# One core, two network blocks at 256 tokens: another division of the first row norm and of the last gate

## The chip, the cores and the metric

The kernel runs on one NeuronCore of a Trainium2 chip. The metric is the device time of one launch in microseconds (us); lower is better. Five engines matter: TensorE (PE, with its weight loads PEld), VectorE (DVE), ScalarE (ACT), GpSimd (POOL) and the queue that issues most transfers (SP).

## The reference, cut to what matters

Two networks run one after the other on x, 256 tokens of 1024 numbers in f32. The first block mixes a stick-breaking attention with a gated recurrence and has a feed-forward part; the second has two layers (gated linear attention, then differential attention), each with a feed-forward part and a gated addition. Only the very first and the very last step are touched by the change:

```python
def rmsnorm(x, g):
    y = x * lax.rsqrt(jnp.mean(x * x, axis=-1, keepdims=True) + EPS)
    return y * g

u = rmsnorm(x, norm1_g) @ w_in                 # the first product
...
gate = sigmoid(rms_norm(h, ple_norm[1]) @ ple_w_gate[1])
out = h + gate * (p[1] @ ple_w_proj[1])        # the last step
```

## The kernel before, in words

**Weights.** All weights are f32 and stream through SBUF in chunks of 128 x 2048 numbers (1 MB), in the order of the list CHUNKS. There are three slots. For each chunk ACT makes a high part (`hi`, L1041, a copy rounded to TensorE's fast format) and DVE a low part (`lo`, L1622, chunk minus high part). Each product is then three: high by high, high by low, low by high (`mm3`, over `mm` at L360). SP reloads a slot when the high and the low part of its old chunk exist (L2432). Chunk 0 comes in four pieces of 128 x 512, chunk 1 in two.

**Activations.** Tokens lie in two blocks of 128 rows. For a product they are turned: PE transposes a 128 x 128 block of each token block into PSUM (`turn_step`, L368), ACT copies the high part of it to X or O (`turn_hi`, L1050) and DVE computes the low part (`turn_lo`, L1634). A chunk's product goes over eight k blocks, each with one turned block.

**Start.** ACT issues the transfers of the identity and of a small table and loads its function table. Meanwhile PE runs 16 warm-up products of the identity with itself (each an f32 product of two loads). When a half of x lands, ACT squares it in two operations of 512 columns with a row sum (`row_square`, L1056; x0 is token block 0, x1 token block 1). The sums go through a ladder of tiny steps between DVE and ACT (`rows_rstd`, `rstd_y`, `rstd_r`; L1660, L1655, L1063, L1065, L1641, L1643, L1645). Then DVE scales token block 0 (L1719) and ACT token block 1 (L1098), the first 512 columns of each; ACT makes the high part of piece 0 of chunk 0, waits for the turning of k block 0, copies it, scales the other 512 columns (L1102), and goes on with copies and pieces in turn. DVE waits for that high part, makes the low part, scales its other 512 columns (L1722), and makes X's low parts.

**End.** The last four chunks are the gate's weights. `toks` computes one chunk: for each k block both token blocks, all in one PSUM bank, 48 products; the semaphore `gemm` rises after the last. ACT then takes the sigmoid of both token blocks (L1447), DVE multiplies with the projected p (L2150) and adds to H (L2152), each in one operation over both token blocks (128 x 512), and SP writes 256 columns of all tokens to the output (L2441), 256 KB.

Each engine's program is written out by hand in its order; a wait holds up everything behind it on its engine.

Of the kernel before, what the change touches and what calls it, by code (L numbers as in the profile page):

```python
# [10 lines left out]
ALU = mybir.AluOpType  # L11
ACT = mybir.ActivationFunctionType
# [170 lines left out]
hg_sig hg_lf hg_kq hg_one hg_ln hg_d hg_acc hg_ed hg_ex hg_p hg_s hg_acc2 hg_o  # L183
gates mg mg_hi mg_lo ff_b ff_ev ff_sq ff_hi ff_lo n1_r pn_r nm1_r bgh fin_m fin_r fin_h
gz gl_qk gl_l gl_m gl_abs gl_one gl_scan gl_c gl_e gl_z gl_s gl_u gl_ua gl_w gl_x gl_o gl_r8 gla_ev
sw_b sw_g sw_u sw_t sw_s sw_w sw_hi sw_lo p_hi p_lo ple_pw ple_g ple_gg ple_h
df_ev df_sq df_r df_kn df_tr df_qk df_sc df_mx df_e df_a df_ta df_at df_o df_l df_lx df_tab df_dsq df_ap df_dt df_thi df_tlo""".split()


# [111 lines left out]
def v3(ap, a):  # L301
    return ap.rearrange("p (a b) -> p a b", a=a)
# [52 lines left out]
def tensor_program(e, m):  # L355
# [88 lines left out]
    def toks(c, bank, ops, norm=None, ks=range(8)):  # L444
        w = m.weights(c)
        if ks[0] == 0:
            ready(c)
        for k in ks:
            if norm:
                ahead(norm, k)  # L450
            for tb in range(2):
                i = mm3(PS[:, bank, tb * 256:tb * 256 + 256], [x[:, k, tb * 128:tb * 128 + 128] for x in ops],
                        [x[:, k, :] for x in w], k == 0 and tb == 0, k == 7, True)
        if ks[-1] == 7:
            i.then_inc(s["gemm"], 1)
# [36 lines left out]


    e.wait_ge(s["d_idn"], 16)
    for _ in range(16):
        mm(PS[:, 3, 0:128], ident, ident, True, True)


# [319 lines left out]
    def swiglu(layer):  # L818
# [3 lines left out]
        for i in range(12):  # L822
# [22 lines left out]
            if i >= 1:  # L845
# [5 lines left out]
                else:  # L851
                    down_last(down_at(layer, 10), half_slot(ring, 10), 0, [4, 5, 6, 7], f"pn{layer}",
                              lambda: e.wait_ge(s["sw_w"], f0 + 11))

    def ple(layer):
        r0 = 16 if layer == 0 else 24
        for n in range(4):
            if n == 1:
                e.wait_ge(s["res"], r0)
            toks(AT[f"ple_w_gate{layer}"] + n, 3 + n, m.pair("OX"[layer]), f"pn{layer}" if n == 0 else None)  # L860
            if layer == 0 and n >= 1:
                h_step("nm1", 2 * n - 2)
                h_step("nm1", 2 * n - 1)
# [164 lines left out]
def scalar_program(e, m):  # L1028
# [58 lines left out]
    e.dma_start(m.CON[:, 0:nc0], m.io["const"][:, 0:nc0]).then_inc(s["d_idn"], 16)  # L1087
    e.dma_start(m.SML[:, 0:8], m.io["small"][:, 0:8]).then_inc(s["d_g1"], 16)
    e.preload_act_table_set(LOGEXP)
    for tb in range(2):  # L1090
        e.wait_ge(s[f"d_x{tb}"], 16)
        for n in range(2):
            row_square("n1", tb, n)
    rstd_y("n1")
    e.wait_ge(s["n1_r"], 1)
    r1 = m.sc("n1.r")[:, 1:2]
    H, HS = m.tok(m.H), m.tok(m.HS)
    act(HS[:, 1, 0:512], H[:, 1, 0:512], ACT.Copy, scale=r1).then_inc(s["n_hsa"], 1)  # L1098
    hi(0, 0)
    e.wait_ge(s["d_g1"], 16)  # L1100
    turn_hi("n1", 0)
    act(HS[:, 1, 512:1024], H[:, 1, 512:1024], ACT.Copy, scale=r1).then_inc(s["n_hsa"], 1)  # L1102
# [333 lines left out]
    def ple(layer):  # L1436
        g, pn, r = v3(m.ar(3584, 2048), 2), f"pn{layer}", m.sc(f"pn{layer}.r")
        new_residual(5 if layer else 3, pn)
        rstd_y(pn)
        e.preload_act_table_set(SIGMOID)  # L1440
        for n in range(4):
            c = AT[f"ple_w_gate{layer}"] + n
            hi(c + 2)
            e.wait_ge(s["gemm"], c + 1)
            e.wait_ge(s["pn_r"], layer + 1)
            for tb in range(2):
                i = act(g[:, tb, 256 * n:256 * n + 256], PS[:, 3 + n, 256 * tb:256 * tb + 256], ACT.Sigmoid,  # L1447
                        scale=r[:, tb:tb + 1])
            i.then_inc(s["ple_g"], 1)
            if layer == 0 and n >= 1:  # L1450
                turn_hi("nm1", 2 * n - 2, 2 * n - 1)
                if n == 2:
                    row_square("nm1", 0, 0)
                    row_square("nm1", 1, 0)
        e.preload_act_table_set(LOGEXP)
# [151 lines left out]
def vector_program(e, m):  # L1607
# [56 lines left out]
    def rows_rstd(name, sem=None):  # L1664
        mean_square(name, rows_sum(name), 1.0 / 1024)
        return rstd_r(name, sem)
# [47 lines left out]
            i.then_inc(s["ns_ap"], 1)  # L1714


    r = rows_rstd("n1", ("n1_r", 1))
    H, HS = m.tok(m.H), m.tok(m.HS)
    e.tensor_scalar(HS[:, 0, 0:512], H[:, 0, 0:512], r[:, 0:1], None, ALU.mult).then_inc(s["n_hsd"], 1)  # L1719
    e.wait_ge(s["d_g1"], 16)  # L1720
    lo(0, 0)
# [417 lines left out]
    def ple(layer, r):  # L2139
        pw, g = m.ar(1536, 2048), m.ar(3584, 2048)  # L2140
        pn = f"pn{layer}"
        new_residual(5 if layer else 3, [4, 5, 6, 7], r)
        rows_rstd(pn, ("pn_r", layer + 1))
        for n in range(4):
            c = slice(256 * n, 256 * n + 256)
            lo(AT[f"ple_w_gate{layer}"] + n + 2)
            gg = v3(g, 2)[:, :, c]
            e.wait_ge(s["ple_pw"], 4 * layer + 4)
            e.wait_ge(s["ple_g"], 4 * layer + n + 1)
            e.tensor_tensor(gg, gg, v3(pw, 2)[:, :, c], ALU.mult).then_inc(own.up(), 1)  # L2150
            settled()
            e.tensor_tensor(H[:, :, c], H[:, :, c], gg, ALU.add).then_inc(s["ple_h"], 1)  # L2152
            if layer == 0 and n >= 1:
                turn_lo("nm1", 2 * n - 2, 2 * n - 1)
# [260 lines left out]
def sync_program(e, m):  # L2415
# [20 lines left out]
            src = io[name][k1 * 128:(k1 + kn) * 128, n0:n0 + nn].rearrange("(k p) n -> p k n", p=128)  # L2436
            e.dma_start(m.chunk(c, j)[0].rearrange("p (k n) -> p k n", k=kn), src).then_inc(s[landed(c, j)[0]], 16)
    o_rows = m.out.rearrange("(b p) d -> p b d", p=128)
    for n in range(4):
        e.wait_ge(s["ple_h"], 5 + n)  # L2440
        e.dma_start(o_rows[:, :, 256 * n:256 * n + 256], H[:, :, 256 * n:256 * n + 256]).then_inc(s["d_out"], 16)  # L2441
    e.wait_ge(s["d_out"], 64)


def program(nc, io, out):
# [74 lines left out]
```

## Time and profile before

| | us |
|---|---|
| median of 3 runs | 1082.48 |
| lowest and highest of them | 1080.42, 1082.62 |
| the profiled execution, its own time | 1080.15 |
| span of the profiled execution, first to last instruction | 1078.0 |
| DMA data read from HBM | 181.8 MB |

All rows that follow are of the one profiled execution; times in them count from the start of its span. The page gives the busy share of each engine and the chain of work that ended last. The chain view lists that chain in order of time: start, length, what. The timeline lists instructions in order: start, length, engine, line, operation, tiles and shapes, number of instructions merged, and in brackets the idle time in front and what ended it. The windows view gives, for each stretch, the busy time and number of instructions of each engine, the granted clock of TensorE (1.00 is full), the share of time in which the transfer engines are busy, and GB/s.

### The profile page before, as it was taken

How to read it: one execution, taken by the hardware profiler on the slowest of the kernel's cores; microseconds unless marked ns; L12 is line 12 of the kernel's file. 1: busy time of each engine (PE TensorE's matmuls, PEld its weight loads, DVE VectorE, ACT ScalarE, POOL GpSimd, SP SyncE). 2: the span in 40 equal slices, each digit the busy share in tenths (PEclk: the TensorE clock that was granted, in tenths of full speed). 3: DMA queues.
4: the chain of work that ended last, by engine and by line, in shares of the span. 5: the costliest groups of instructions: out<-in, count | busy, mean ns of one | idle time of the engine just before them, and what ended most of it. 6: DMA issues, size and time to landing. Idle time of an engine off the chain costs nothing.

```text
span 1078.0 us, 16570 instructions
## 1 busy us (share of the span) xinstructions
PE 1058.2 (98%) x6790; PEld 949.2 (88%) x6790; DVE 714.5 (66%) x819; ACT 598.7 (56%) x764; POOL 48.2 (4%) x51
## 2 busy tenths in 40 slices
PE   7999999999999999999999999999999999999998
PEld 7999999888888879998888888899998888888888
DVE  5557776756565666866566666667989676666564
ACT  6557544464444446756654544476686564444464
POOL 0000000020000000000102300010000100000010
PEclk9999999999999999999999999999999999999999
DMA  7835434546556455345455554645533446555641
GB/s 258 260 119 171 143 119 156 176 152 203 192 174 217 160 176 178 117 158 166 157 196 185 205 195 159 212 152 172 173 112 119 161 164 200 187 196 172 215 160 40
DMA packets 138298, 183.93 MB, mean 171 GB/s; under 512 B 4176, under 2 KB 122064, under 8 KB 138224
## 3 DMA queue, kind: packets, MB, share of 16 engines
q1 hardware_dynamic: 137776, 182.29, 50.9%
q8 instruction: 54, 0.88, 0.3%
q0 software_dynamic: 160, 0.52, 0.2%
q14 instruction: 20, 0.16, 0.0%
q10 hardware_dynamic: 288, 0.07, 0.0%
HBM read 181.82 MB, written 1.05 MB: 170 GB/s over the span
## 4 chain that ended last, share of the span: by engine, by line
PE 91%; DVE 4%; ACT 2%; issue 1%; DMA 1%; ACTq 0%; SPq 0%; DVEq 0%
PE PS L360 89%; PE PS L368 2%; DVE WL L1622 1%; ACT WH L1041 1%; DMA RAW<-in_gla_w_in_dram 0%; DMA H<-in_x_dram 0%; ACT HS L1056 0%; ACT AR L1056 0%; DVE SC L2212 0%; DVE HS L1711 0%; ACT SC L1063 0%; ACT SC L1065 0%; ACT X L1050 0%; DVE SC L1655 0%; DVE AR L2150 0%
## 5 line engine op out<-in xcount | busy, mean ns | idle before, releaser
L1622 DVE TENSOR_TENSOR WL<-RAW,WH 128x2048 fp32r<-128x2048 f32 (+1 forms) x170 | 379.0, 2231 | 149.8 <-ACT WH L1041 149.3
L1041 ACT ACTIVATE WH<-RAW 128x2048 fp32r<-128x2048 f32 (+1 forms) x175 | 325.5, 1863 | 92.4 <-PE PS L360 88.8
L360 PE MATMUL PS<-WH,X 128*128 128x256 f32 (+1 forms) x1264 | 312.0, 333 | 0.7 <-issue 0.5
L360 PE MATMUL PS<-O,WH 128*128 128x512 f32 (+2 forms) x880 | 265.3, 362 | 0.7 <-DVE AR L2012 0.7
L360 PEld LDWEIGHTS PS<-WH,X 128*128 128x128 f32 x1264 | 216.7, 190 | 24.8 <-issue 1.3
L360 PE MATMUL PS<-X,WH 128*128 128x256 f32 (+1 forms) x864 | 218.0, 331 | 1.8 <-DVE X L1634 1.0
L360 PE MATMUL PS<-WL,X 128*128 128x256 f32 (+1 forms) x632 | 208.8, 330 | 0.0
L360 PE MATMUL PS<-O,WL 128*128 128x256 f32 x744 | 203.2, 281 | 0.0
L360 PEld LDWEIGHTS PS<-O,WH 128*128 128x128 f32 (+1 forms) x880 | 155.0, 187 | 25.5 <-DVE AR L2012 0.9
L360 PE MATMUL PS<-X,WL 128*128 128x256 f32 x608 | 167.5, 281 | 0.0
L360 PEld LDWEIGHTS PS<-X,WH 128*128 128x128 f32 x864 | 144.9, 190 | 16.8 <-ACT X L1050 1.2
L360 PE MATMUL PS<-WH,O 128*128 128x256 f32 (+1 forms) x624 | 149.3, 327 | 0.6 <-issue 0.6
L360 PEld LDWEIGHTS PS<-O,WL 128*128 128x128 f32 x744 | 140.0, 188 | 3.1
L360 PEld LDWEIGHTS PS<-WL,X 128*128 128x128 f32 x632 | 120.0, 190 | 11.3
L360 PEld LDWEIGHTS PS<-X,WL 128*128 128x128 f32 x608 | 115.3, 190 | 1.8
L360 PEld LDWEIGHTS PS<-WH,O 128*128 128x128 f32 x624 | 105.6, 190 | 10.0 <-ACT O L1520 0.7
L360 PE MATMUL PS<-WL,O 128*128 128x256 f32 (+1 forms) x312 | 101.1, 324 | 0.0
L1410 ACT ACTIVATE AR<-PS 128x512 f32<-128x512 f32 x44 | 26.3, 597 | 116.3 <-PE PS L360 116.3
L360 PEld LDWEIGHTS PS<-WL,O 128*128 128x128 f32 x312 | 59.4, 190 | 4.7
L360 PE MATMUL PS<-AR 128*128 128x128 f32 (+7 forms) x512 | 59.2, 300 | 1.4 <-ACT AR L1504 1.1
L360 PEld LDWEIGHTS PS<-AR 128*128 128x128 f32 (+3 forms) x512 | 50.2, 177 | 6.8 <-issue 1.8
L2368 POOL TENSOR_TENSOR WL<-RAW,WH 128x2048 fp32r<-128x2048 f32 x5 | 23.1, 4620 | 533.6 <-ACT WH L1041 533.6
(197 smaller groups left out, 774.2 us busy)
## 6 DMA issues: line engine op xcount, KB each, us to landing
RAW<-in_ffn_w_in_dram SPq DMA_DIRECT2D x44, 1024.0 KB, 5.1
RAW<-in_w_ff_dram SPq DMA_DIRECT2D x32, 1024.0 KB, 5.4
RAW<-in_ffn_w_out_dram SPq DMA_DIRECT2D x22, 1024.0 KB, 5.1
RAW<-in_w_in_dram SPq DMA_DIRECT2D x20, 1024.0 KB, 5.1
RAW<-in_gla_w_in_dram SPq DMA_DIRECT2D x12, 1024.0 KB, 5.5
RAW<-in_diff_w_in_dram SPq DMA_DIRECT2D x12, 1024.0 KB, 5.2
RAW<-in_ple_w_gate_dram SPq DMA_DIRECT2D x8, 1024.0 KB, 5.2
RAW<-in_w_out_dram SPq DMA_DIRECT2D x4, 1024.0 KB, 5.0
```

Of the source, the lines that this page charges most:

```text
L360: return e.matmul(o, l, r, start=start, stop=stop, skip_group_check=skip)
L368: return e.transpose(o, i, m.con("ident", slice(0, k))[:, 0:k])
L1041: act(high, raw, ACT.Copy).then_inc(s["w_hi"], 1)
L1410: act(v3(m.ar(5632 + 1024 * x + 512 * (i % 2), 512), 2), PS[:, 2 * x:2 * x + 2, 256:512], ACT.Copy).then_inc(s["sw_b"], 1)
L1622: e.tensor_tensor(low, raw, high.bitcast(F32), ALU.subtract).then_inc(s["w_lo"], 1)
L2368: e.tensor_tensor(low, raw, high.bitcast(F32), ALU.subtract).then_inc(s["w_lop"], 1)
```

## The change

It has four parts at the start and one at the end.

1. PE runs 10 warm-up products instead of 16.
2. ACT squares only token block 0. DVE squares token block 1 in two operations (H x 1.0 x H with a row sum) once x1 has landed, waits for its own results, and goes into the ladder.
3. ACT makes the high part of piece 0 of chunk 0 after its last step of the ladder and in front of the scaling, where it came behind the scaling.
4. The last gate chunk of the last layer (n == 3) is computed by token block: all eight k blocks of token block 0 into bank 6, then of token block 1 into bank 7. A new semaphore, ple_t, rises after the first. Each block has its own sigmoid, its own product and addition of 256 columns on DVE, and its own output transfer of 128 KB. ACT's last table load falls away.

```diff
@@ tensor
     e.wait_ge(s["d_idn"], 16)
-    for _ in range(16):
+    for _ in range(10):
         mm(PS[:, 3, 0:128], ident, ident, True, True)
+    def last_gates():
+        c, ops = AT["ple_w_gate1"] + 3, m.pair("X")
+        w = m.weights(c)
+        ready(c)
+        for tb in range(2):
+            for k in range(8):
+                i = mm3(PS[:, 6 + tb, 0:256], [x[:, k, 128 * tb:128 * tb + 128] for x in ops],
+                        [x[:, k, :] for x in w], k == 0, k == 7)
+            i.then_inc(s["ple_t" if tb == 0 else "gemm"], 1)
@@ scalar
-    for tb in range(2):
-        e.wait_ge(s[f"d_x{tb}"], 16)
-        for n in range(2):
-            row_square("n1", tb, n)
+    e.wait_ge(s["d_x0"], 16)
+    ss = m.sc("n1.ss")
+    act(m.tok(m.HS)[:, 0, 0:512], m.tok(m.H)[:, 0, 0:512], ACT.Square, accum_out=ss[:, 0:1])
+    act(m.tok(m.HS)[:, 0, 512:1024], m.tok(m.H)[:, 0, 512:1024], ACT.Square, accum_out=ss[:, 2:3]).then_inc(s["row_sq"], 1)
     rstd_y("n1")
+    hi(0, 0)
     e.wait_ge(s["n1_r"], 1)
...
     act(HS[:, 1, 0:512], H[:, 1, 0:512], ACT.Copy, scale=r1).then_inc(s["n_hsa"], 1)
-    hi(0, 0)
...
+            if layer == 1 and n == 3:
+                for tb in range(2):
+                    e.wait_ge(*((s["gemm"], c + 1) if tb else (s["ple_t"], 1)))
+                    act(g[:, tb, 768:1024], PS[:, 6 + tb, 0:256], ACT.Sigmoid, scale=r[:, tb:tb + 1]).then_inc(s["ple_g"], 1)
+                return
@@ vector
+    H, HS = m.tok(m.H), m.tok(m.HS)
+    e.wait_ge(s["d_x1"], 16)
+    for n in range(2):
+        c = slice(512 * n, 512 * n + 512)
+        e.scalar_tensor_tensor(out=HS[:, 1, c], in0=H[:, 1, c], scalar=1.0, in1=H[:, 1, c], op0=ALU.mult, op1=ALU.mult,
+                               accum_out=m.sc("n1.ss")[:, 2 * n + 1:2 * n + 2]).then_inc(own.up(), 1)
+    settled()
     r = rows_rstd("n1", ("n1_r", 1))
...
+            if layer == 1 and n == 3:
+                for tb in range(2):
+                    gg = v3(g, 2)[:, tb, c]
+                    e.wait_ge(s["ple_g"], 8 + tb)
+                    e.tensor_tensor(gg, gg, v3(pw, 2)[:, tb, c], ALU.mult).then_inc(own.up(), 1)
+                    settled()
+                    e.tensor_tensor(H[:, tb, c], H[:, tb, c], gg, ALU.add).then_inc(s["ple_h"], 1)
+                return
@@ sync
-    for n in range(4):
+    for n in range(3):
         e.wait_ge(s["ple_h"], 5 + n)
         e.dma_start(o_rows[:, :, 256 * n:256 * n + 256], H[:, :, 256 * n:256 * n + 256]).then_inc(s["d_out"], 16)
-    e.wait_ge(s["d_out"], 64)
+    for b in range(2):
+        e.wait_ge(s["ple_h"], 8 + b)
+        e.dma_start(o_rows[:, b, 768:1024], H[:, b, 768:1024]).then_inc(s["d_out"], 16)
+    e.wait_ge(s["d_out"], 80)
```

## Rows read from the trace of the kernel before

**Rows 1.** The page: busy time by engine; the chain by engine.
```profile
PE 1058.2 (98%) x6790; PEld 949.2 (88%) x6790; DVE 714.5 (66%) x819; ACT 598.7 (56%) x764; POOL 48.2 (4%) x51
...
PE 91%; DVE 4%; ACT 2%; issue 1%; DMA 1%; ACTq 0%; SPq 0%; DVEq 0%
```

**Rows 2.** The chain view, 0 to 30 us: start, length, what.
```profile
6.22 1.34 ACT HS L1056 x4
...
7.59 0.17 DVE SC L1660
...
9.76 0.53 ACT WH L1041
...
10.42 0.69 DVE WL L1622
...
11.51 0.41 DVE X L1634
...
12.01 0.95 PE PS L360 x6
...
18.53 1.24 DVE WL L1622
```

**Rows 3.** Windows view of the start, and the timeline of PE's weight loads.
```profile
5.00:8.20 3.20, 3.18 (x15) 3.18 (x16) 0.33 (x2) 2.70 (x9) 0.00 (x0) 1.00 1.07 358
8.20:10.10 1.90, 1.90 (x19) 1.90 (x19) 0.97 (x4) 1.26 (x3) 0.00 (x0) 1.00 1.10 354
10.80:12.00 1.20, 0.22 (x2) 0.02 (x1) 1.11 (x3) 1.20 (x3) 0.00 (x0) 1.00 1.10 347
...
5.02 5.15 PEld L360 LDWEIGHTS PS<-CON 128*128 128x128 f32 x32 [5.02 <-DMA CON<-in_const_dram]
10.09 0.69 PEld L368 LDWEIGHTS PS<-CON,HS 128*128 128x128 f32 x6
...
12.70 0.24 PEld L368 LDWEIGHTS PS<-CON,HS 128*128 128x128 f32 x2
```

**Rows 4.** Timeline of ACT at the start.
```profile
5.97 0.19 ACT L1056 ACTIVATION_READ_ACCUMULATOR HS<-H 128x1 f32 x1
...
9.04 0.72 ACT L1098 ACTIVATE HS<-H,SC 128x512 f32<-128x512 f32 x1 [0.62 <-DVE SC L1645]
9.67 0.61 ACT L1041 ACTIVATE WH<-RAW 128x512 fp32r<-128x512 f32 x1
10.69 0.47 ACT L1050 ACTIVATE X<-PS,SML 128x256 fp32r<-128x256 f32 x1 [0.40 <-PE PS L368]
...
13.21 0.47 ACT L1050 ACTIVATE X<-PS,SML 128x256 fp32r<-128x256 f32 x1 [0.20 <-PE PS L368]
```

**Rows 5.** Timeline of DVE at the start.
```profile
11.03 0.48 DVE L1722 TENSOR_SCALAR HS<-H,SC 128x512 f32<-128x512 f32 x1
```

**Rows 6.** DVE's groups by line and shape: count, busy us, mean ns, idle before.
```profile
L1973 DVE SCALAR_TENSOR_TENSOR AR<-AR 128x512 f32<-128x512 f32 x16 | 11.1, 692 | 0.5
...
L1783 DVE TENSOR_TENSOR O<-PS,O 128x256 fp32r<-128x256 f32 x4 | 1.7, 416 | 0.2 <-ACT O L1155 0.2
```

**Rows 7.** Timelines of ACT and DVE at the end.
```profile
1067.31 0.84 ACT L1447 ACTIVATE AR<-PS,SC 128x256 f32<-128x256 f32 x2 [4.92 <-PE PS L360]
1073.07 0.84 ACT L1447 ACTIVATE AR<-PS,SC 128x256 f32<-128x256 f32 x2 [4.92 <-PE PS L360]
...
1074.73 0.69 DVE L2152 TENSOR_TENSOR H<-H,AR 128x512 f32<-128x512 f32 x1
```

**Rows 8.** Transfers, 1074 to 1078: GB/s in 0.1 us slices; issues with time to landing.
```profile
GB/s 0 0 0 0 0 0 0 0 0 0 0 0 0 0 0 0 0 0 0 0 0 0 0 113 358 348 328 338 369 348 307 113 0 0 0 0 0 0 0 0
...
out_dram<-H SPq DMA_DIRECT2D x1, 256.0 KB, 2.1
```

**Rows 9.** Transfers issued from 1.6 to 2.0 us.
```profile
RAW<-in_w_in_dram SPq DMA_DIRECT2D x1, 256.0 KB, 5.3
```

**Rows 10.** Waits of SP over the whole span: us in total, times, longest.
```profile
SPq L2432 <- DVE WL L1622: 935.7, 163, 15.6
```

More of the change, by code:

```diff
@@ L185 @@
 gz gl_qk gl_l gl_m gl_abs gl_one gl_scan gl_c gl_e gl_z gl_s gl_u gl_ua gl_w gl_x gl_o gl_r8 gla_ev
-sw_b sw_g sw_u sw_t sw_s sw_w sw_hi sw_lo p_hi p_lo ple_pw ple_g ple_gg ple_h
+sw_b sw_g sw_u sw_t sw_s sw_w sw_hi sw_lo ple_t p_hi p_lo ple_pw ple_g ple_gg ple_h
 df_ev df_sq df_r df_kn df_tr df_qk df_sc df_mx df_e df_a df_ta df_at df_o df_l df_lx df_tab df_dsq df_ap df_dt df_thi df_tlo""".split()
@@ L859, in ple @@
                 e.wait_ge(s["res"], r0)
+            if layer == 1 and n == 3:
+                last_gates()
+                break
             toks(AT[f"ple_w_gate{layer}"] + n, 3 + n, m.pair("OX"[layer]), f"pn{layer}" if n == 0 else None)
@@ L1714, in norm_apply @@
             i.then_inc(s["ns_ap"], 1)
+    H, HS = m.tok(m.H), m.tok(m.HS)
[5 more added lines that the diff above has]
+    settled()
     r = rows_rstd("n1", ("n1_r", 1))
-    H, HS = m.tok(m.H), m.tok(m.HS)
     e.tensor_scalar(HS[:, 0, 0:512], H[:, 0, 0:512], r[:, 0:1], None, ALU.mult).then_inc(s["n_hsd"], 1)
@@ L2146, in ple @@
             lo(AT[f"ple_w_gate{layer}"] + n + 2)
+            if layer == 1 and n == 3:
+                for tb in range(2):
[5 more added lines that the diff above has]
+                return
             gg = v3(g, 2)[:, :, c]
```

## The prediction, made before the change was run

> **What bounds the kernel now.** I read the page first: PE is busy for 98% of the span, and the chain that ended last lies on PE for 91% of it [rows 1]. DVE (66%) and ACT (56%) have slack almost everywhere. So a microsecond can only be won where PE does not yet run or no longer runs, and this change touches those two places and no other. Then I read the chain of the first 30 us [rows 2]. PE's first product comes at 12.01. What leads there is the transfer of x (its second half is there at 6.22), ACT's squares, a ladder of tiny steps that ends at 9.04, the scaling of the rows (0.72) [rows 4], the high part of the first weight piece, its low part (10.42 to 11.11), DVE's second scaling and the first low part of the turned X (until 11.92). Two more things must be seen there, which the chain does not show. The 32 loads of the 16 warm-up products occupy PE from 5.02 until 10.17, and the first turning of X stands behind them at 10.09 [rows 3], although the later of the two scaled halves was there at 9.04 + 0.72 = 9.76 [rows 4]. And ACT, once it has scaled and copied the first high part, waits 0.40 us for that turning [rows 4].
>
> Last I read the end. The final gate chunk is through when ACT starts on it at 1073.07; then come two sigmoids, a product and an addition on DVE over both token blocks, and one 256 KB transfer [rows 7, 8]. From there to the end of the span are 1078.0 - 1073.07 = 4.93 us without a product, which nothing hides.
>
> **Terms at the start.** (a) Fewer warm-up products. Per product there are two loads. In the windows [rows 3] the loads begin 0.21 us apart until 8.2 and 0.11 us apart after it: 3.2 us / 15 intervals, and 1.9 us for 17 loads and a part of the turning. The granted clock of both windows reads 1.00, so the record does not show the change of level; the pace says 1.2 GHz ahead of 8.2 and 2.4 GHz behind it. 20 loads instead of 32: sixteen have begun by 8.2 (to 8.18, at 0.21), four more at 0.11 are through at about 8.75. PE is then free 1.4 us earlier, and the turning starts when the scaled halves are there.
>
> (b) Squares of token block 1 on DVE. Now ACT needs 1.34 us for them after 6.22 [rows 2]. On DVE an operation with two f32 inputs of 512 columns out of SBUF takes 0.69 us (L1973) [rows 6]. Operations of that kind follow one another every 0.6 us: 10.42 to 11.03 between the low part and the scaling [rows 2, 5]. Two make 0.61 + 0.69 = 1.30. No row of before shows DVE with a sum output, so the cost of that is bounded: nothing at the low end, 0.19 us each at the high end (ACT's own read of its sum [rows 4]). I take 0.08 each, half of a tiny DVE step of 0.17 [rows 2], since such a step is the nearest DVE row and half of it may overlap. That gives 6.22 + 1.30 + 0.16 = about 7.7, against 7.59 now: the ladder begins 0.1 us **later** (bounds -0.05 and +0.35). The move takes ACT off the path and puts DVE on it; it gains nothing by itself. Nothing else is queued on DVE at that time, and ACT finishes the other half at 5.97 + 0.19 = 6.16 [rows 4], hidden behind the arrival of x.
>
> One rule of the Trainium skill speaks against it. Our row shows a two-input f32 operation at 0.69 us, the full pace of one column per 1.07 ns. The Vector Engine (DVE) Microarchitecture Reference, section Points that are easy to get wrong, says that this kind of operation with two SBUF sources that aren't bf16 halves its throughput, because both read ports are taken. L1973 contradicts that without a sum; no row has it with one. It is a rival below.
>
> (c) The high part before the scaling. ACT idles 0.62 us ahead of the scaling; the copy takes 0.61 [rows 4] and the first weight piece has landed at about 1.7 + 5.3 = 7.0 [rows 9]. It fits into that hole, so it costs nothing and the scaling is not pushed back. It lets DVE make the low part right behind its scaling (9.5 to 10.2 instead of 10.42 to 11.11), and takes 0.6 us of DVE work away from before the first low part of X. If the hole were gone, it would cost at most 0.61.
>
> Sum at the start. The scaled halves are there at 9.76 + 0.1 = 9.86. In steady state ACT's copy of a turned block starts 0.5 us after the first load of that turning begins (12.70 to 13.21) [rows 3, 4]. So ACT starts at about 10.4 instead of 10.69: 0.3 earlier. The first product could come 0.5 earlier (X's low part is 10.9 to 11.4 instead of until 11.92). But behind it ACT runs scaling, copy, high part and copy with no wait between them: its next idle row is the one at 13.21 [rows 4]. That stretch begins with the copy at 10.69 and so moves by 0.3 only, and DVE's low parts follow it. So the third k block starts 0.3 earlier, and from there on PE's own pace decides. Gain at the start: **0.3 us** (bounds 0 from b's high end, 0.6 if the first product decides). It is kept until the end: chunk 1 waits for its low part, which DVE makes at 18.53 behind the last turned block [rows 2], SP waits for DVE's low parts before it reloads a slot (163 waits) [rows 10], and all of that shifts along.
>
> **Terms at the end.** The last chunk has the same 48 products at the same size, only sorted by token block; consecutive gates start 5.76 us apart (1067.31 and 1073.07) [rows 7], so each half is 2.88 us and PE ends as now. Token block 0's tail (below 2 us of ACT and DVE, then its transfer) starts at 1070.2 and lies beside the second half. Behind it remain: one sigmoid of 0.47 instead of the pair of 0.84, saving 0.37; a product and an addition of 256 columns, where the nearest row has 0.42 (L1783) [rows 6], instead of 0.69 each [rows 7], saving 2 x 0.27 = 0.54; and a transfer of half the size. The data of the 256 KB transfer move for eight slices of 0.1 us; issue to landing is 2.1 us [rows 8]. Half the bytes save up to 0.4, at least 0 if more than the moving was fixed; I take 0.4, because the eight slices run at a full 340 GB/s. Together 0.37 + 0.54 + 0.4 = **1.3 us** (bounds 0.9 and 1.3). The added wait of DVE on the second sigmoid has nothing queued behind it but its own two operations; SP's fifth output transfer waits behind the fourth, which is issued 2.9 us ahead and landed by then. The dropped table load (1.28 us, ends before the transfer) was hidden. DMA: Bandwidth & Descriptors in the Trainium skill, section Anatomy of one DMA, says most of a transfer's fixed part is the confirmation from the target and does not depend on size; 2.1 less 0.8 of moving agrees, and by that the saving is the moving part alone.
>
> **Sum.** 0.3 + 1.3 = 1.6 us. On the profiled execution: span 1078.0 - 1.6 = 1076.4, its own time 1080.15 - 1.6 = 1078.5 (2.15 us lie outside the span). The median of the runs is 1082.48, so 2.3 above the profiled one, though the lowest run, 1080.42, is close to it. Carried to the median: 1082.5 - 1.6 = **1080.9 us**. Less than 0.2% (2.2 us) cannot be told from no change here, and 1.6 is below it.
>
> **Rivals.**
> 1. *Clock rises later in most runs.* The end of 32 warm-up loads depends on when the pace changes, and the program does not choose that. At 0.21 throughout, they would end at 5.02 + 32 x 0.213 = 11.84 instead of 10.17, and the turning with them; 20 loads would end at 9.3, still before the scaled rows at 9.86. Each run of before in which the rise is late loses up to 1.7 more, the kernel after almost nothing. For it: three runs spread over 2.2 us, the profiled one lies at the bottom. Against: other work of a long kernel varies too, and late slow products cost both. Gain 1.6 to 3.3; with 3.3, 1079.2. Chance 0.36.
> 2. *DVE squares at half pace* (the skill's rule of above as a mechanism of this kernel). Each square would take 1.3 instead of 0.7, the ladder begins 1.25 late, all of the start with it: scaled rows at 11.0, product 0.6 later than before. 0.6 lost against 1.3 at the end: 0.7 gain, 1081.8. For it, only the rule; against it L1973 at 0.69. Chance 0.08.
> 3. *The end gives less than it says*: transfer of 128 KB as slow as 256 KB, or a wait of some tenths between the halves: 0.9 + 0.3, 1081.3. Chance 0.08.
> 4. *PE's clock falls back, and it gets slower.* Between 8.75 and the first product at 11.5 PE would do only the six turning loads (0.7 us). If it goes to 1.2 GHz there, a product of 256 columns costs about 0.23 instead of 0.12 (5.76 us / 48), by the ratio 0.21 to 0.11 of the loads: 0.11 lost each. A low stretch of 3.2 us as at the beginning eats 1.5 (1082.4, par); from 15 products on it is slower than before, from 34 on (3.8 us lost) by over 0.2%; all of chunk 0 gives 5.3 lost, 1086. Against it: between 10.8 and 12.0 PE does 0.22 us of work now and the products behind run at full pace. Chance 0.05.
>
> **How the numbers follow.** Forecast 0.43, rivals 0.36, 0.08, 0.08, 0.05. The forecast's own range is 1080.3 to 1081.9 (bounds of b and of the transfer); a tenth of its weight falls past 1080.3. Faster by over 0.2% (under 1080.3): 0.36 plus 0.05 = 0.41. Slower by over 0.2%: 0.05. Same: 0.54. The range that leaves out 2 in 10 cuts the outer part of rival 1 and all of rival 4: 1078.7 to 1082.3.
>
> **What would show it.** Right: 20 loads ending near 8.8, the turning's first load near 9.9, DVE's two squares over by 7.7, first product near 11.5, last sigmoid's start to end of span 3.6 to 3.7 instead of 4.93, and five output transfers of which the last is 128 KB. Wrong: squares of more than 0.75 each, the high part ending after the ladder, loads of 0.2 behind 12, a gap on PE between the last two halves, or a last transfer that takes 2.1 again.

## Result and profile after

| | kernel before | changed kernel |
|---|---|---|
| median of the runs, us | 1082.39 (20 runs, 1080.23 to 1083.93) | 1080.31 (19 runs, 1078.62 to 1080.70) |
| ratio of the changed kernel, 95% interval | | 0.9982 (0.9975 to 0.9989) |
| the profiled execution, its own time | 1080.15 | 1080.1 |
| its span | 1078.0 | 1078.0 |

One further run of the changed kernel took 2691 us and is left out. The gain is 2.08 us of the median (0.18%; by the interval 1.2 to 2.7 us). The prediction had 1080.9, and the interval leaves 1 out, though the gain is below the 0.2% that the prediction took to be the least that can be told from no change. Yet the two profiled executions are equally long, and that needs an explanation: by the steps of the prediction the span should have been 1.6 us shorter.

The page of the changed kernel, busy time by engine, stands beside [rows 1]. DVE has 1.6 us more, with its squares, and ACT 2.5 less. PE is busy 1.0 us **more** although it has twelve warm-up instructions less, which is a first sign that some of its products took longer.

```profile
PE 1059.2 (98%) x6778; PEld 949.9 (88%) x6778; DVE 716.1 (66%) x825; ACT 596.2 (55%) x759; POOL 48.2 (4%) x51
```

The chain of the changed kernel, 0 to 30 us (start, length, what), against [rows 2]:

```profile
6.87 0.70 DVE HS L1740 x3
...
7.60 0.17 DVE SC L1679
...
9.05 0.73 ACT HS L1113
...
9.92 0.42 PE PS L368 x2
...
10.43 0.48 ACT X L1064
...
11.53 0.94 PE PS L360 x6
```

The first product starts at 11.53 instead of 12.01. In PE's timeline the third k block starts at 13.69 instead of 13.95, and chunk 1 at 19.66 instead of 19.90: between these two executions the start has gained 0.24 us. The ladder begins at 7.60, where it was 7.59. The timelines of its engines show why (start, length, engine, line, operation, in brackets the idle time in front and what ended it): PEld, ACT, DVE.

```profile
5.05 4.26 PEld L360 LDWEIGHTS PS<-CON 128*128 128x128 f32 x20 [5.05 <-DMA CON<-in_const_dram]
9.89 0.64 PEld L368 LDWEIGHTS PS<-CON,HS 128*128 128x128 f32 x6 [0.57 <-DVE HS L1744]
```
```profile
8.34 0.61 ACT L1055 ACTIVATE WH<-RAW 128x512 fp32r<-128x512 f32 x1
9.05 0.72 ACT L1113 ACTIVATE HS<-H,SC 128x512 f32<-128x512 f32 x1
10.43 0.47 ACT L1064 ACTIVATE X<-PS,SML 128x256 fp32r<-128x256 f32 x1 [0.66 <-PE PS L368]
```
```profile
6.25 0.69 DVE L1740 SCALAR_TENSOR_TENSOR HS<-H 128x512 f32<-128x512 f32 x1 [6.25 <-DMA H<-in_x_dram]
6.87 0.08 DVE L1740 DVE_READ_ACCUMULATOR HS<-H 128x1 f32 x1
6.87 0.68 DVE L1740 SCALAR_TENSOR_TENSOR HS<-H 128x512 f32<-128x512 f32 x1
7.48 0.08 DVE L1740 DVE_READ_ACCUMULATOR HS<-H 128x1 f32 x1
```

PE no longer stands in front of the turning: it idles 0.57 us until the scaled rows exist. The loads took 0.21 us each nearly to the end here, so in this execution the clock rose about 1 us later than in that of [rows 3]. The high part (L1055) lies in the hole before the scaling. The squares take 0.69 and 0.68, each with 0.08 for its sum.

The end: the timelines of ACT and DVE, and the last transfer (issue to landing), against [rows 7, 8].

```profile
1071.56 0.47 ACT L1461 ACTIVATE AR<-PS,SC 128x256 f32<-128x256 f32 x1 [2.04 <-PE PS L360]
1074.43 0.47 ACT L1461 ACTIVATE AR<-PS,SC 128x256 f32<-128x256 f32 x1 [2.40 <-PE PS L360]
```
```profile
1074.94 0.43 DVE L2176 TENSOR_TENSOR AR<-AR 128x256 f32<-128x256 f32 x1 [1.99 <-ACT AR L1461]
1075.40 0.42 DVE L2178 TENSOR_TENSOR H<-H,AR 128x256 f32<-128x256 f32 x1
```
```profile
out_dram<-H SPq DMA_DIRECT2D x1, 128.0 KB, 1.7
```

From the last sigmoid to the end of the span are 1078.0 - 1074.43 = 3.57 us instead of 4.93: 1.36 gained. So 0.24 + 1.36 = 1.6 us are gained at the two ends, and yet the last sigmoid starts 1074.43 - 1073.07 = 1.36 us **later** than before. The middle, which the change does not touch, has lost 1.6 us. The windows view (busy time and number of instructions of PE, PEld, DVE, ACT, POOL, then granted clock, share of the transfer engines, GB/s) finds most of it, here for the changed kernel and then for the one before:

```profile
183.80:185.80 2.00, 0.20 (x2) 0.12 (x2) 2.00 (x5) 0.00 (x0) 0.00 (x0) 1.00 0.36 33
186.00:187.00 1.00, 1.00 (x9) 0.93 (x8) 0.34 (x1) 0.85 (x2) 0.00 (x0) 0.84 0.93 385
187.00:188.00 1.00, 1.00 (x7) 1.00 (x7) 0.54 (x2) 0.02 (x1) 0.00 (x0) 0.50 1.02 422
188.00:190.00 2.00, 2.00 (x11) 2.00 (x11) 1.06 (x2) 1.08 (x1) 0.00 (x0) 0.50 0.21 80
190.00:191.00 1.00, 1.00 (x10) 1.00 (x10) 0.28 (x2) 0.84 (x1) 0.00 (x0) 0.95 0.00 0
```
```profile
183.80:185.80 2.00, 0.35 (x3) 0.14 (x2) 2.00 (x5) 0.00 (x0) 0.00 (x0) 1.00 0.25 35
...
188.00:190.00 2.00, 2.00 (x19) 2.00 (x18) 1.28 (x2) 1.72 (x1) 0.00 (x0) 1.00 0.32 121
```

In both executions PE has almost nothing to do from 183.8 to 185.8: it waits 1.80 us for a low part of O that stands in DVE's program behind a weight chunk's low part (L1641 in the changed kernel). In the changed kernel's execution the granted clock then goes to 0.50 (1.2 GHz) from within the slice 186 to 187 until past 190 (0.16 / 0.5 + 3 + 0.05 / 0.5 = 3.4 us by the rows); 11 products go through in two microseconds instead of 19. DVE's operation L1943, which takes the next result, stands at 195.29, where its counterpart (L1918 of the kernel before) stands at 194.05: 1.24 later, though the start was 0.24 earlier. That is a loss of 1.48 us in this stretch; 0.12 are spread over the rest.

### The profile page after: what moved, and what is told of

The parts are those of the page before. It is cut to its first block, busy times and chain, and to the rows that moved or that the text cites. A ratio compares the mean times of both kernels' runs of the same rounds, so it can differ in the third digit from the quotient of the medians.

```text
span 1078.0 us, 16547 instructions
## 1 busy us (share of the span) xinstructions
PE 1059.2 (98%) x6778; PEld 949.9 (88%) x6778; DVE 716.1 (66%) x825; ACT 596.2 (55%) x759; POOL 48.2 (4%) x51
## 4 chain that ended last, share of the span: by engine, by line
PE 91%; DVE 4%; ACT 2%; issue 1%; DMA 1%; SPq 0%; DVEq 0%; ACTq 0%
PE PS L360 89%; PE PS L368 2%; DVE WL L1641 1%; ACT WH L1055 1%; DMA RAW<-in_gla_w_in_dram 0%; DMA H<-in_x_dram 0%; ACT AR L1070 0%; DVE SC L2245 0%; ACT X L1064 0%; DVE HS L1730 0%; ACT SC L1077 0%; ACT SC L1079 0%; DVE SC L1674 0%; DVE H L2185 0%; DVE AR L2183 0%
## 5 line engine op out<-in xcount | busy, mean ns | idle before, releaser
L1641 DVE TENSOR_TENSOR WL<-RAW,WH 128x2048 fp32r<-128x2048 f32 (+1 forms) x170 | 379.0, 2231 | 148.1 <-ACT WH L1055 147.7
L1055 ACT ACTIVATE WH<-RAW 128x2048 fp32r<-128x2048 f32 (+1 forms) x175 | 325.6, 1863 | 94.5 <-PE PS L360 89.8
```

The lines of the kernel that those rows point to most:

```text
L1055: act(high, raw, ACT.Copy).then_inc(s["w_hi"], 1)
L1641: e.tensor_tensor(low, raw, high.bitcast(F32), ALU.subtract).then_inc(s["w_lo"], 1)
```

## Experiments

All are edits of the changed kernel, and ratios are to the kernel before, timed on the same chip. Beside the median I give how the runs lie, since they lie in **groups** mostly 1.2 to 2.2 us apart, with the mean granted clock of the execution: the kernel before has them at about 1080.3 (clock 0.999 to 1.000), 1082.5 (0.997 to 0.998) and 1083.5 (0.997), the changed kernel at 1078.7 (5 of 19 runs, 1.000) and 1080.3 (14 of 19, 0.998). A mean of 0.999 need not be a low stretch among the products: in the kernel before's profiled execution the only one is behind PE's last product (0.57 from 1076 us on). Where two kernels are compared below, equal groups are compared. The experiments ran apart from the changed kernel's runs, on three chips; the kernel before ran beside each of them and has its fastest group at 1079.8 to 1080.7 every time.

### Start alone, end alone

e1 has the changed start and the old end; e2 the old start and the changed end.

```diff
# e1: the end back
-            if layer == 1 and n == 3:
-                last_gates()
-                break
...
# e2: the start back
-    for _ in range(10):
+    for _ in range(16):
...
```

> Only the parts at the start are made (10 warm-up products, squares of token block 1 on VectorE, the high part ahead of the scaling); the end is that of before. My theory: the gains add up and the start is the small one: 0.2 to 0.4 us under before among runs of equal mean granted clock, last sigmoid to end of span 4.93 as before. Rival (the late rise of the clock makes before's upper runs, which fewer warm-ups cure): 0.3 under before in its lower runs and 1.5 to 2 under it in its upper runs, so the start alone would give most of the 2.1 us by which the medians differ.

> Only the end is made (last gate chunk by token block, each with its own tail and transfer); the start is that of before. My theory: 1.3 us under before (0.9 on ACT and DVE, 0.4 on the transfer) among runs of equal mean granted clock; last sigmoid to end of span 3.6. The runs still fall into two groups some 1.7 to 2 us apart. Rival (clock at the start): 1.3 under before too, but then this kernel alone keeps an upper group as frequent as before's.

Measured: **e1** 1080.46 (12 runs), ratio 0.9990 (0.9981 to 0.9998); 8 runs at 1080.1 to 1080.5, 4 at 1081.5 to 1082.0. **e2** 1081.29 (11 runs), ratio 0.9993 (0.9984 to 1.0003); 2 runs at 1078.6 and 1079.2, 8 at 1080.8 to 1081.8, 1 at 1082.4. The kernel before on the same chip has 11 runs at 1079.9 to 1080.6, 13 at 1082.0 to 1082.9 and 3 at 1083.4 to 1083.6. PEld and ACT at the start, for e1 and then e2:

```profile
5.11 4.34 PEld L360 LDWEIGHTS PS<-CON 128*128 128x128 f32 x20 [5.11 <-DMA CON<-in_const_dram]
9.95 1.11 PEld L368 LDWEIGHTS PS<-CON,HS 128*128 128x128 f32 x6 [0.51 <-DVE HS L1736]
...
10.74 0.47 ACT L1061 ACTIVATE X<-PS,SML 128x256 fp32r<-128x256 f32 x1 [0.91 <-PE PS L368]
```
```profile
5.04 6.27 PEld L360 LDWEIGHTS PS<-CON 128*128 128x128 f32 x32 [5.04 <-DMA CON<-in_const_dram]
11.23 0.69 PEld L368 LDWEIGHTS PS<-CON,HS 128*128 128x128 f32 x6
...
11.83 0.47 ACT L1064 ACTIVATE X<-PS,SML 128x256 fp32r<-128x256 f32 x1 [1.53 <-PE PS L368]
```

The 32 loads of 16 warm-up products took 6.27 us in e2 and 5.15 in [rows 3], with the same program up to there. So the moment at which the clock rises is not the program's: that was the premise of rival 1, and it holds. In both of these executions it came late: the 20 loads of e1 took 0.21 us each to the end, and its six turning loads 1.11 us instead of 0.64. Then the first product starts at 12.92 in e2 and at 11.84 in e1, and chunk 1 at 21.05 and 19.97, 1.08 apart both times. With the rise at about 8.2 the kernel before has 12.01 and 19.90; with the rise at about 9.2 the changed kernel has 11.53 and 19.66. So fewer warm-up products protect against most of a late rise, not all of it: e1's chunk 1 is 0.07 later than that of the kernel before with its early rise.

The runs say the same of the start alone. e1's expectation of 0.2 to 0.4 us in equal groups fails in the fastest one: e1's runs (1080.1 to 1080.5) lie where those of the kernel before lie. In the next group they are about 0.8 lower. The end alone is 1.1 and 1.7 lower in e2's two fastest runs and about 1.1 in the next group. The end is worth what was said: from the last sigmoid to the end of the span are 1079.2 - 1075.63 = 3.6 us in e2 and 1078.4 - 1073.46 = 4.9 in e1.

### The parts of the start, one undone at a time

```diff
# e4_warm_16
-    for _ in range(10):
+    for _ in range(16):
# e7_warm_0
-    for _ in range(10):
+    for _ in range(0):
# e5_squares_back: ACT squares both token blocks, DVE none
-    e.wait_ge(s["d_x0"], 16)
...
+    for tb in range(2):
+        e.wait_ge(s[f"d_x{tb}"], 16)
+        for n in range(2):
+            row_square("n1", tb, n)
# e6_piece_back
-    hi(0, 0)
     e.wait_ge(s["n1_r"], 1)
...
     act(HS[:, 1, 0:512], H[:, 1, 0:512], ACT.Copy, scale=r1).then_inc(s["n_hsa"], 1)
+    hi(0, 0)
```

> The changed kernel with 16 warm-up products again. My theory: in an execution whose clock rises early (loads at 0.11 us from about 8.2) the 32 loads end near 10.2, the turning starts 0.3 late and the first product comes at 11.8 to 11.9 instead of 11.5. In one whose clock rises late, at 10.5 or after, the loads end at 11.3, and the first product comes at 12.9 as in the kernel with the end alone. Rival (the number of warm-up products doesn't matter because the scaled rows are late anyway): first product at 11.5 whenever the clock rises.

> The changed kernel without any warm-up product. It tells what the clock does to a start without them (my rival 4 in its strongest form). If the clock does not rise before the products: turning loads and the products of chunk 0 at half pace, 0.23 instead of 0.12 a product, for about 3 to 5 us, so the third k block starts 1 us later or more and the end 1.5 to 2.5 us later. If the clock were up anyway, nothing changes but PE's idle time ahead of 9.9.

> The changed kernel with all four squares on ACT again. My theory, after the changed kernel's trace (VectorE's squares were over at 7.56, as ACT's before): nothing moves; first tiny step at 7.59 to 7.60, turned copy at 10.4, first product at 11.5. My prediction of before had VectorE 0.1 later than ACT, by which this kernel would be 0.1 earlier. The high part of piece 0 is not pushed, because ACT is free from 7.6 on.

> The changed kernel with the high part of piece 0 behind the scaling again. My theory: ACT's turned copy still starts near 10.4, VectorE's low part of piece 0 goes back to 10.4 to 11.1 and its second scaling behind it, X's first low part to 11.4, first product near 12.0; but the third k block moves by 0.1 or less, because ACT's stretch behind the first copy is the same. So the last product comes 0 to 0.2 later. Rival (the low part is what leads): the whole 0.5 us is lost until the end.

| | median us (runs) | ratio, interval | chunk 1's first product in the profile |
|---|---|---|---|
| changed kernel | 1080.31 (19) | 0.9982 (0.9975 to 0.9989) | 19.66 |
| e4, 16 warm-up products | 1081.35 (8) | 0.9993 (0.9982 to 1.0004) | 20.33 |
| e7, none | 1080.86 (8) | 0.9993 (0.9982 to 1.0004) | 20.25 |
| e5, squares back on ACT | 1079.92 (8) | 0.9978 (0.9967 to 0.9989) | 19.86 |
| e6, high part back | 1079.77 (6) | 0.9985 (0.9971 to 1.0000) | 19.81 |

**e4**: its fastest group, 1079.3 and 1079.4, is 0.6 above the changed kernel's, its middle one (1081.1 to 1081.4) 0.9 above, and three runs at 1082.3 to 1082.5 lie in a third that the changed kernel lacks. The turning starts at 10.51, right behind the 32nd load, and the first product at 12.20. **e7**: without warm-up products the turning is in time (9.70), but six loads take 1.14 instead of 0.64 and the first products 0.63 a pair instead of 0.40, until about 13.3; the third k block and chunk 1 come 0.6 later, where 1 us or more was expected. Its runs are 4 at 1080.4 to 1080.6 (clock 0.999 to 1.000) and 4 at 1081.1 to 1081.6 (0.998), 1.8 and 0.9 above the changed kernel's groups; no row shows where the part of this that exceeds 0.6 is lost. Of the three numbers tried, ten lie between a queue that is too long and an engine that is still at half clock. **e5**: the ladder began at 7.63 in its profile, where the changed kernel has 7.60; the fastest runs, 1078.2 and 1078.8, lie by the changed kernel's. The 0.2 at chunk 1 belongs to a slower turning (0.81 for six loads), not to the squares. Moving the squares to DVE brings nothing and costs nothing that these runs resolve. **e6**: the low part of the first piece is at 10.39 instead of 9.46, the first product at 11.97, chunk 1 at 19.81, and the fastest group at 1078.8 to 1079.2: the moved high part is worth 0.15 us at chunk 1, up to 0.4 in the runs. (Its median is low because three of its six runs fell into the fastest group, where five of 19 did of the changed kernel; with so few runs a median says how they fell, and groups must be compared.)

### The last transfer in one piece

```diff
# e8_one_transfer
-    for n in range(3):
-        e.wait_ge(s["ple_h"], 5 + n)
+    for n in range(4):
+        e.wait_ge(s["ple_h"], 5 + n + (n == 3))
...
-    for b in range(2):
-        e.wait_ge(s["ple_h"], 8 + b)
-        e.dma_start(o_rows[:, b, 768:1024], H[:, b, 768:1024]).then_inc(s["d_out"], 16)
```

> The changed kernel with the last 256 columns of both token blocks written by one 256 KB transfer again, behind the second block's addition. My theory: issue to landing 2.1 instead of 1.7 us, span 0.4 longer, all else equal. Rival (the tail's end does not hang on the size of the transfer): span unchanged within 0.1.

Measured: 1080.74 (8 runs), ratio 0.9992 (0.9980 to 1.0004). Its groups are at 1079.2 and 1080.7, each 0.4 to 0.5 above those of the changed kernel, and two runs are at 1082.2. The profile says the same: its last transfer,

```profile
out_dram<-H SPq DMA_DIRECT2D x1, 256.0 KB, 2.1
```

lands after 2.1 instead of 1.7, and the last sigmoid is 1078.6 - 1074.61 = 3.99 us ahead of the end instead of 3.57. So the half transfer is worth 0.4 of the 1.36, and the halves of sigmoid, product and addition the rest.

### The pause at 184 us: removed, and filled

In the changed kernel DVE makes the low part of chunk w0 + 25 in front of the low parts that PE waits for. e3 puts it behind them; e10 does so also at 401 us, where PE waits another 1.80 us behind a chunk's low part. e9 leaves the pause at 184 and lets PE run seven products of the identity in it; e11 fills both pauses. The filling products go to a PSUM bank that nobody reads then. In e10 `new_residual` makes the low part (`between`) behind its second addition and turning.

```diff
# e3_low_part_later
-    lo(w0 + 25)
...
     turn_lo("ohg", 0, 1, 2, 3)
+    lo(w0 + 25)
# e10_both_low_parts, besides
-        if i >= 1:
+        if 1 <= i < 16:
             lo(ff_down_at(i - 1) + 2)
-    new_residual(1, [4, 5, 6, 7], q)
+    new_residual(1, [4, 5, 6, 7], q, lambda: lo(ff_down_at(15) + 2))
# e9_fill_7
+        if k == 3:
+            for _ in range(7):
+                mm(PS[:, 3, 0:128], ident, ident, True, True)
# e11_fill_both, besides e9
+                    if norm == "nm0":
+                        for _ in range(7):
+                            mm(PS[:, 3, 0:128], ident, ident, True, True)
```

> The changed kernel, with one step of VectorE moved: the low part of the second w_o_hg chunk comes behind the four low parts of the turned recurrence output instead of in front of the gates. PE's 1.8 us pause at 184 us should go down to under 0.3, because PE there waits for a low part that stands behind 2.3 us of other VectorE work. My theory: the runs' two groups come from a fall of the granted clock right behind this pause, so with the pause the upper group goes: all runs at a mean clock of 1.000, 1.5 to 1.8 us under the changed kernel's lower group (1078.7), near 1077.0, and 3 us under its median. Rival (the groups come from the moment of the clock's rise at the start): two groups remain, both 1.5 to 1.8 lower.

> The changed kernel, with seven extra products of the identity (14 loads, 1.6 us) put into PE's pause at 184 us; they go to a bank that nobody reads. The pause stays as long as it was. My theory: no fall of the clock at 186.7, all runs at a mean clock of 1.000 and at the changed kernel's lower group, 1078.7 to 1079. Rival (groups made at the start): two groups as in the changed kernel, 1078.7 and 1080.4. A third possibility, that the extra products delay the turning: 0.1 to 0.3 more.

> The changed kernel with two steps of VectorE moved: the one at 184 us as in the kernel with the low part later (1.8 us of PE pause gone there), and at 401 us the last low part of the feed-forward weights between the second and the third residual addition instead of in front of the first. PE's pause of 1.8 us at 401 should shrink to under 0.5; some of it comes back as a wait of 0.8 to 1 us in front of the first product of the next stage, whose turned low part now stands behind that low part. My theory (a fall of the granted clock follows a pause of this kind, at 184 or at 401): without both pauses all runs are at a mean clock of 0.999 to 1.000, one group, near 1075.7. Rival (falls come whatever the pauses): groups 1.7 apart remain as with one pause removed.

> The changed kernel with seven extra products of the identity in each of the two pauses, at 184 and at 401 us; the pauses stay as long as they are. My theory: no clock falls behind either, one group of runs at 1078.6 to 1079.1, none at 1080 or above. Rival (falls come whatever PE does there): two or three groups, as with the first pause filled alone (1079.0, 1080.2, 1081.5).

Measured (the groups with their mean granted clock):

| | median us (runs) | ratio, interval | fastest group, clock 0.999 to 1.000 | next group, 0.998 | slowest, 0.997 to 0.998 |
|---|---|---|---|---|---|
| e3 | 1077.41 (6) | 0.9959 (0.9946 to 0.9972) | 1076.5 to 1076.7 (3) | 1078.2, 1078.4 | 1079.7 |
| e10 | 1077.19 (5) | 0.9955 (0.9941 to 0.9969) | 1075.9, 1076.0 | 1077.2 | 1078.5, 1078.6 |
| e9 | 1080.12 (9) | 0.9981 (0.9971 to 0.9991) | 1079.0 (4) | 1080.1 to 1080.4 (4) | 1081.5 |
| e11 | 1080.98 (11) | 0.9988 (0.9978 to 0.9998) | 1079.2 to 1079.5 (4) | 1080.9 to 1081.0 (3) | 1082.2 to 1083.1 (4) |

e3 beats both kernels. The view of waits (engine, line and releaser, us in total, times, longest) has the two pauses in the changed kernel, one in e3, none in e10, where 0.6 us come back at 401 in front of another product:

```profile
PE PS L368 <- DVE H L1699: 1.8, 1, 1.8
PE PS L368 <- DVE O L1653: 1.8, 1, 1.8
```
```profile
PE PS L368 <- DVE H L1699: 1.8, 1, 1.8
```
```profile
PE PS L360 <- DVE O L1653: 0.6, 1, 0.6
```

The fastest group moves by 1078.7 - 1076.5 = 2.2 us, rather more than the pause of 1.8. So 1.8 us of idle PE were on the path, whatever the clock did. The second pause gives 0.6 more, half of the 1.8 - 0.6 = 1.2 that the waits show. That the filled pause costs no less than the empty one (e9's fastest runs at 1079.0, 0.2 to 0.3 above the changed kernel's) is as it should be: the products wait for DVE, not for PE. But **the groups stay** in all four. They are not made by these two pauses alone. e11's profiled execution is of its slowest group, and the windows view shows it at half clock elsewhere, from 436.0 to 442.8:

```profile
432.80:436.00 3.20, 3.20 (x16) 2.69 (x15) 1.75 (x4) 1.91 (x1) 0.00 (x0) 1.00 0.69 240
436.00:437.00 1.00, 1.00 (x3) 0.34 (x2) 0.59 (x2) 0.37 (x1) 0.00 (x0) 0.51 0.00 0
437.00:442.00 5.00, 5.00 (x24) 4.97 (x24) 4.86 (x6) 4.87 (x6) 0.00 (x0) 0.50 0.00 0
```

e5's profile has such a fall at the same place:

```profile
437.00:440.00 3.00, 3.00 (x17) 3.00 (x16) 3.00 (x4) 2.94 (x4) 0.00 (x0) 0.50 0.03 5
```

What PE did ahead of it is not a pause: the profile has it busy all the time, with 16 products that have only 32 rows of weights (the gates; 14 of them are in this view by form, 430 to 436 us of e11: count, busy us, mean ns, idle before).

```profile
L360 PE MATMUL PS<-AR 32*128 32x256 f32 x14 | 3.3, 386 | 0.0
```

These products alone do not make the clock fall either. The kernel before runs the same 16 in the same place, and its clock stays up (windows of the kernel before):

```profile
432.80:436.00 3.20, 3.20 (x16) 2.77 (x16) 1.89 (x5) 1.91 (x1) 0.00 (x0) 1.00 0.82 282
437.00:442.00 5.00, 5.00 (x44) 5.00 (x43) 4.97 (x7) 4.87 (x6) 0.00 (x0) 1.00 0.08 10
```

### The gates' products apart

This is e10 with half a chunk's products between the two groups of gate products, so that the 32-row products do not stand in one row.

```diff
# e13_gates_apart, besides e10
     gates(0)
+    gin(4, range(4))
     gates(1)
-    for n in range(4, 8):
+    gin(4, range(4, 8))
+    for n in range(5, 8):
         gin(n)
```

> Changed from the changed kernel: the low part of w0 + 25 goes behind the turning of chunk hg, and that of the last feed-forward piece of chunk 1 goes in between two residual additions (both as in e10_both_low_parts), and TensorE takes a half of the last chunk between the two groups of gate products instead of all 17 loads of 32-row products in one row. Theory: the groups of times 1.2 to 1.7 us apart come from stretches of half clock (1.2 GHz), which in two of the profiled executions (e5_squares_back and e11_fill_both) began at 436 to 437 us, just behind these 32-row products. If they are what the granted clock falls behind in the slower executions of e10_both_low_parts too (1077.2 and 1078.6 beside 1075.9), then with the products apart all executions lie together near 1075.9 at a mean granted clock of 1.000, and the ratio to the kernel before is 0.994. Rival: the falls of those executions come from other pauses of TensorE (1.1 us at 821 us, 0.8 us at 19 us), and the groups stay: 1075.9, 1077.2 and 1078.6, ratio 0.9955. Second rival: the order costs by itself, the gates' values coming later to VectorE: the fastest group then moves up by 0.3 us or more, to 1076.3 or later.

Measured: 1079.92 (11 runs), ratio 0.9980 (0.9971 to 0.9989): 2 runs at 1078.3 and 1078.6 (clock 1.000), 9 at 1079.6 to 1080.3 (0.998). The theory fails in both halves. The groups stay, and the fastest is 2.4 above e10's: the second rival, with a larger price than it named. The gates' values now come later to DVE, and a chunk's low part behind them comes later to PE (timeline of PE, then the windows around it):

```profile
453.20 0.36 PE L360 MATMUL PS<-WH,O 128*128 128x256 f32 x1 [2.09 <-DVE WL L1643]
```
```profile
452.00:453.00 1.00, 0.00 (x0) 0.00 (x0) 1.00 (x2) 1.00 (x1) 0.00 (x0) 1.00 0.00 0
...
454.00:455.00 1.00, 1.00 (x9) 1.00 (x8) 1.00 (x2) 0.78 (x1) 0.00 (x0) 0.73 0.58 93
455.00:456.00 1.00, 1.00 (x7) 1.00 (x6) 1.00 (x2) 1.00 (x2) 0.00 (x0) 0.50 0.95 317
```

The edit made a new pause of 2.09 us, and within the slice that begins 0.8 us after its end the clock fell. It fell nowhere near 436. So this run can't say whether 32-row products in a row make the clock fall, since it put a pause in their place. It does show a fall behind a pause, at a place where no other profiled execution has one.

## Why the prediction came out as it did

**What bounds the kernel: right for PE, wrong for the places.** The prediction said that a microsecond can only be won where PE does not yet run or no longer runs. e3 took 2.2 us out of the middle, where PE waited 1.80 us in an otherwise full program.

**(a) Fewer warm-up products: right** in mechanism. PE is free before the scaled rows exist, and the turning starts at 9.89, for which the prediction had 9.86. The end of the loads was forecast at 8.75 and came at 9.31, since the clock rose later than in the kernel before's execution; it cost nothing here, as the scaled rows came only behind that. e4 puts the price of the old number at 0.6 to 0.9 us with everything else changed, for an execution in which the 32 loads took 5.58 us.

**(b) Squares on DVE: right.** 0.69 and 0.68 with 0.08 for each sum; the ladder begins at 7.60, where 7.7 was forecast, since the first sum is read beside the second square. The rule of the Trainium skill against it (Vector Engine (DVE) Microarchitecture Reference, section Points that are easy to get wrong) does not show in these rows: with a sum output the operation takes as long as L1973 does without [rows 6]. (The pace of 1.07 ns a column that the prediction names is an estimate; by L1973 and L1783 it is (692 - 416) / 256 = 1.08.) Rival 2 is refuted, and e5 shows no worth of the part alone.

**(c) High part in front: right.** It costs nothing, as it ends before the scaling starts, and brings the low part 0.96 us forward (9.46). e6 gives the worth in the sum: 0.15 us at chunk 1.

**Sum at the start: right for the profiled pair**, 0.24 measured against 0.3. The first product came 0.48 earlier, the third k block 0.26, as was argued: ACT's row of copies decides. But it is no fixed number. It hangs on when the clock rises in each of the two executions: at chunk 1, e1 is 0.07 behind the kernel before's profiled execution and 1.08 ahead of e2, which has the old start and a late rise. In the fastest group of runs e1 shows no gain of the start at all.

**The end: right**, 1.36 against 1.3. e8 isolates the term of the transfer that had bounds 0 and 0.4: it is 0.4. That it goes with the bytes fits the page DMA: Bandwidth & Descriptors of the Trainium skill, section Anatomy of one DMA, which describes a transfer issued by GpSimd, not by SP as here, and puts most of a fixed part of about 2.0 us into the confirmation. The prediction could not know from one size that 1.3 of the 2.1 us are fixed; with two sizes it comes out as an estimate, 1.7 - 0.4 = 1.3 us. That is less than the page's figure, and the measurement decides. Rival 3 is refuted. The wait between the halves did not come: PE had no gap there.

**From the profile to the median: right in size, incomplete in reason.** 1082.39 - 1.6 is 1080.8, and 1080.31 was measured, at the edge of the forecast's own range. The gain of 2.08 also lies in the 1.6 to 3.3 of rival 1, so the medians do not tell the two apart. The prediction left the 2.3 us between the profiled execution and the median of before unexplained. By the mean clock of its slower runs (0.997 to 0.998) they come from half-clock stretches in the middle, which the profiled one lacks. The changed kernel has them too: its profiled execution has one and the kernel before's has none, so 1.6 us gained and 1.6 lost gave the same span. The difference of two profiled executions would have said that the change does nothing.

**Rival 1: its mechanism is real, but it is not alone what spreads the runs.** A late rise costs the old start 1.08 us more in e2 than the new one in e1, and the prediction was right to price it. It had the changed kernel lose almost nothing by it; e1's chunk 1 is 0.31 later than the changed kernel's. It does not make the groups alone, for they are there in all kernels with ten warm-up products as well. Its part may be read from the groups: the fastest of both kernels are 1080.3 - 1078.7 = 1.6 apart, the forecast's figure, and the next 1082.5 - 1080.3 = 2.2. That the additional 0.6 is the late rise is argued, not shown.

**Rival 4, the clock falls back: not where it was placed.** Between the warm-up loads and the first product no profiled execution with warm-up products shows it: some are still at the low clock in the turning (e1), but the products behind run at full pace in all. But a low stretch in the middle costs what this rival reckoned for one at the start: 1.5 us.

**What stays open** is what decides in which execution the clock falls. Of nine profiled executions with the 1.80 us pause at 184 us unfilled, four fell behind it (the changed kernel, e2, e7, e8) and five did not (before, e1, e4, e5, e6). Two fell at 436 us without a pause in front (e5, e11), one behind the new pause of e13. Programs that are the same at that place do either. And not every pause of this length is followed by a fall: the one at 401 us, also 1.80 us long, stands unfilled in eleven profiled executions (these nine, e3 and e9), and none fell behind it. Nor do the 32-row products alone bring a fall, as the kernel before shows. The page TensorE: Matmul & The Clock Gate of the Trainium skill, section What's actually happening, says that the chip's monitor runs freely against the program, so that the same kernel has more or fewer of its first products at the low clock from run to run. The differing ends of the warm-up loads agree with that, and four falls of nine could have the same reason. A fall behind 3.2 us in which PE reads busy 1.00 is not explained by it, and no run here settles it.

## What to carry to other kernels

Where a kernel is bound by one engine at 98%, count its idle time at the two ends first, and then its longest waits in the middle: the two pauses of 1.8 us, each from one low part that stood too early in DVE's program, took another 2.8 us off the fastest group (1078.7 to 1075.9), where all parts of this change together took 1.6 (1080.3 to 1078.7). The ratio to the kernel before is 0.9982 with the change and 0.9955 with both. Compare the granted clock over the whole span before you compare two spans, and compare medians of many runs by group: one execution against another can hide 1.6 us or invent them. Size warm-up work so that it ends when the data arrive, by its slowest pace.

## What the runs showed of the hardware

- The rise of TensorE's clock has no fixed moment: 20 loads of warm-up took 3.75 (e10), 3.80 (e6), 4.26 (changed kernel) and 4.34 us (e1), and 32 took 5.15, 5.58 (e4) and 6.27 us (e2). The record of the granted clock reads 1.00 throughout these stretches; only the pace of the loads shows it.
- In a long kernel with PE busy for 98%, the granted clock still falls to 0.50 for some 3.4 us at a time (6.8 in e11). By the mean clock of the runs most executions have such a stretch. In the changed kernel's profile it cost 1.48 us; neighbouring groups of runs are mostly 1.2 to 2.2 us apart. It followed the pause of 1.8 us at 184 us in four of nine profiled executions, the equally long one at 401 us in none of eleven, and it came twice without a pause (e5, e11).
- A transfer of the output from SP's queue took 1.7 us for 128 KB and 2.1 for 256 KB.
- DVE squared 512 f32 columns with a row sum in 0.69 us, as long as an operation of two inputs without a sum (L1973), and read the sum in 0.08 us, the first time beside the next square; ACT's read of its sum took 0.19 [rows 4].
